# Parameter rows loaded in pairs, and late rounding, roots, evictions and table loads moved in a two-block transformer kernel

## The reference

```python
# first block, for each layer l
h = rmsnorm(x, g_mix[l]);  proj = h @ w_in[l]           # 1024 -> 6656
# proj: gates, a gated 31-tap convolution, and three attentions (neighbourhood, dilated, windowed)
x = x + sum(sigmoid(gate + gate_b) * (y_n @ w_branch[l, n]) for n in range(4)) @ w_out[l]
u = depthwise_conv(rmsnorm(x, g_ffn[l]) @ w_up[l]);     x = x + (silu(gate) * up) @ w_down[l]
# second block, for each layer l; cs is a second stream of 256 context tokens
m = silu(c) @ w_mod[l] + b_mod[l]                       # 1024 -> 9216, one row for x, one for cs
x, cs = half ffn step, modulated by m[0:3]
p = modulate(rmsnorm(x, mix_norm[l]), m[3:6]) @ w_in[l] # Fourier part, 3-tap conv part, q, kv, rope
x = x + m[5] * (concat(fourier, conv, latent attention over x and cs) @ w_out[l])
x = half ffn step, modulated by m[6:9]                  # cs likewise, but not in the last layer
```

## Time and profile before

| | |
|---|---|
| median of 3 runs | 2647.29 us (2644.49 to 2649.88) |
| the profiled execution's own time | 2649.91 us |
| its span in the trace | 2648.1 us |
| TensorE (PE) busy | 2568.1 us, 97% |
| VectorE (DVE) busy | 1483.0 us, 56% |
| ScalarE (ACT) busy | 1028.8 us, 39% |
| GpSimd (POOL) busy | 55.1 us, 2% |
| mean granted clock of TensorE | 0.994 of 2.4 GHz |

### The profile page before, as it was taken

How to read it: one execution, slowest core, us unless ns; L and a number is a source line. 1 busy time by engine, 2 the same in 40 slices (tenths; PEclk the granted TensorE clock), 3 DMA queues, 4 the chain that set the end, 5 groups by cost and what they waited for, 6 DMA issues and landing times.

```text
span 2648.1 us, 48248 instructions
## 1 busy us (share of the span) xinstructions
PE 2568.1 (97%) x20320; PEld 2263.5 (85%) x20320; DVE 1483.0 (56%) x2156; ACT 1028.8 (39%) x1408; POOL 55.1 (2%) x76
## 2 busy tenths in 40 slices
PE   7999999999999999999999999999999999998999
PEld 6998999899899978888876688888888888876999
DVE  6787786777878653333525563333553334545656
ACT  4545564545455432222324432122332122345433
POOL 2003000000100000000000000000000000000000
PEclk8999999999999999999999999999999999999999
DMA  8577766667675642532436342432532532556673
GB/s 222 169 243 175 210 179 184 194 204 211 192 209 166 198 113 85 144 91 76 145 87 185 111 123 80 133 103 71 143 97 87 144 86 81 168 157 188 173 202 118
DMA packets 613848, 393.66 MB, mean 149 GB/s; under 512 B 47470, under 2 KB 609428, under 8 KB 613539
## 3 DMA queue, kind: packets, MB, share of 16 engines
q1 hardware_dynamic: 610623, 383.31, 50.0%
q0 software_dynamic: 2176, 6.42, 1.0%
q10 hardware_dynamic: 868, 1.31, 0.2%
HBM read 389.94 MB, written 1.05 MB: 148 GB/s over the span
## 4 chain that ended last, share of the span: by engine, by line
PE 89%; DVE 6%; ACT 2%; issue 1%; POOL 1%; DMA 1%; DVEq 1%; ACTq 0%
PE acc L1002 12%; PE acc L1004 12%; PE acc L1003 12%; PE scores L1002 6%; PE scores L1003 6%; PE scores L1004 6%; PE scores L1065 3%; PE scores L1066 3%; PE scores L1067 3%; PE acc L1065 3%; PE acc L1066 3%; PE acc L1067 3%; PE stat L1195 2%; DVE hf L2171 1%; DVE wlo L2091 1%
## 5 line engine op out<-in xcount | busy, mean ns | idle before, releaser
L1541 ACT ACTIVATE whi<-raw 128x2048 fp32r<-128x2048 f32 (+3 forms) x346 | 569.0, 1647 | 824.5 <-PE acc L1004 251.3
L2091 DVE TENSOR_TENSOR wlo<-raw,whi 128x2048 fp32r<-128x2048 f32 (+2 forms) x306 | 629.0, 2056 | 214.1 <-ACT whi L1541 213.3
L1002 PE MATMUL acc<-h,whi 128*128 128x512 f32 (+1 forms) x988 | 355.1, 359 | 8.0 <-DVE u L2692 4.6
L1004 PE MATMUL acc<-h,wlo 128*128 128x512 f32 (+1 forms) x988 | 353.1, 357 | 1.6 <-issue 1.6
L1003 PE MATMUL acc<-h,whi 128*128 128x512 f32 (+1 forms) x988 | 353.1, 357 | 0.0
L1002 PE MATMUL acc<-h_hi,whi 128*128 128x256 f32 x1056 | 302.0, 286 | 2.9 <-DVE cg L2573 1.6
L1003 PE MATMUL acc<-h_lo,whi 128*128 128x256 f32 x1056 | 295.8, 280 | 0.0
L1004 PE MATMUL acc<-h_hi,wlo 128*128 128x256 f32 x1056 | 295.5, 280 | 0.0
L1002 PEld LDWEIGHTS acc<-h,whi 128*128 128x128 f32 x988 | 186.9, 189 | 38.9 <-DVE u L2692 5.3
L1002 PE MATMUL scores<-h,whi 128*128 128x512 f32 (+1 forms) x608 | 219.0, 360 | 1.0 <-DVE wlo L2091 1.0
L1003 PE MATMUL scores<-h,whi 128*128 128x512 f32 (+1 forms) x608 | 218.9, 360 | 0.0
(11 more groups left out here) (395 smaller groups left out, 5192.9 us busy)
## 6 DMA issues: line engine op xcount, KB each, us to landing
raw<-in_ffn_w_in_dram SPq DMA_DIRECT2D x176, 512.0 KB, 5.1
raw<-in_w_mod_dram SPq DMA_DIRECT2D x72, 1024.0 KB, 5.3
raw<-in_w_in_dram SPq DMA_DIRECT2D x62, 1024.0 KB, 5.6
raw<-in_w_up_dram SPq DMA_DIRECT2D x88, 512.0 KB, 5.1
raw<-in_ffn_w_out_dram SPq DMA_DIRECT2D x64, 704.0 KB, 4.7
raw<-in_w_down_dram SPq DMA_DIRECT2D x32, 704.0 KB, 4.7
raw<-in_w_out_dram SPq DMA_DIRECT2D x16, 1024.0 KB, 7.2
raw<-in_w_branch_dram SPq DMA_DIRECT2D x16, 512.0 KB, 6.3
```

Of the source, the lines that this page charges most:

```text
L1002: pe.matmul(bank, wh, hi[:, c0 + k, 0:width], start=(k == 0), stop=False)
L1004: ins = pe.matmul(bank, wl, hi[:, c0 + k, 0:width], start=False, stop=(k == ph.shape[0] - 1))
L1541: return act.activation(out_, in_, ACT.Copy, **kw)
L2091: dve.tensor_tensor(wlo[:, s % 2, 0:el], raw[:, slot, 0:el], f32(whi[:, s % 2, 0:el]), ALU.subtract).then_inc(s_lo, 1)
```

## The change

The parameter arrays are loaded for both layers in one DMA (`both`), in another order of rows; the six pairs of head gains (64 wide) are loaded with both halves and both layers in one DMA. Block 0 now holds exactly 128 rows of 8 loads. The third unit of the phases behind a norm (e = 2) is rounded and subtracted in two halves, as the first was before, and so is the unit of 2.1.kv. The sum of squares of the very first norm is made whole on VectorE, which saves TensorE two matmuls. The rest moves instructions: the places of modulation units, `IN_AMONG`, the eviction of 2.x.in's unit 2 in the last layer, the wait of q01, the Silu of `cond`, `load_sqrt`, the root of the kv norm, and the `rpb` loads of layer 1, which now wait until tile 16 of 1.0.up. Cut to its core:

```diff
-MID_MODS = ((2, 2, 1), (2, 2))
-PAIR_MODS = ((2, 0, 2, 0, 2, 0, 0, 0, 0, 0, 0, 0, 2, 1), (2, 0, 2, 0, 1, 0, 0, 0, 2, 1))
+MID_MODS = ((3, 2, 1), (2, 2))
+PAIR_MODS = ((2, 0, 2, 0, 1, 0, 0, 0, 0, 0, 0, 0, 3), (2, 0, 2, 0, 1, 0, 0, 0, 3))
+TAIL_MODS = 2
-IN_AMONG = (9, 12, 15)
+IN_AMONG = (8, 11, 14)
+        self.halved = {0: True, 2: n > 2} if self.behind_norm else {0: name == f"2.{DEPTH - 1}.kv"}
...
+    def both(k, view):
+        ap = A[k].rearrange(view, p=P)
+        first, each = sum(r.shape[0] for r in rows), ap.shape[0] // DEPTH
+        for l in range(DEPTH):
+            column[(k, l)] = first + l * each
+        rows.append(ap)
...
@@ gpsimd @@
+                if l:
+                    pool.wait_ge(s_accfree, by_name[f"1.{l - 1}.up"].t0 + 16)
                 base = A["na_rpb"][l]
...
@@ tensor @@
+                    elif free is not None:
+                        pe.wait_ge(s_accfree, free)
...
-                pe.wait_ge(s_accfree, by_name[nm + "q01"].t0)
-                unit(nm + "q01", 0, None, h2_hi, h2_lo, T, plain(256))
+                unit(nm + "q01", 0, None, h2_hi, h2_lo, T, plain(256), free=by_name[nm + "in"].t0 + 6)
...
                         pair_weigh(k - 2, pairs[k - 2])
+                    given = SITES["pair", l, k] if k < len(pairs) else []
+                    for lu in given:
+                        mod_unit(*lu)
                     if 0 <= k - 1 < len(pairs):
                         pair_turn(k - 1, pairs[k - 1])
-                    for lu in SITES.get(("pair", l, k), []):
-                        mod_unit(*lu)
+                    if k == len(pairs):
+                        for lu in SITES["pair", l, k][:TAIL_MODS]:
+                            mod_unit(*lu)
+                for lu in SITES["pair", l, len(pairs)][TAIL_MODS:]:
+                    mod_unit(*lu)
...
@@ scalar @@
-                if e == 0 and to.behind_norm:
+                if to.halved.get(e):
...
-                load_sqrt()
                 for j in range(DC):
                     round_next(name, j, None)
+                    if j == 0:
+                        load_sqrt()
...
                     if e + DC == IN_AMONG[2]:
+                        act.wait_ge(s_pad2, 2 * (l + 1))
+                        in_out(2)
                         round_next(nm + "in", 3, None)
...
-                take_root(kv_norm)
                 for seg in range(nseg):
...
+                    if seg == 0:
+                        take_root(kv_norm)
...
@@ vector @@
-            dve.tensor_tensor(wlo[:, 0, 0:half], raw[:, 0, 0:half], ...).then_inc(s_head_lo, 1)
+            head_low(0)
+            flatten(norm_x(1, ("g_mix", 0), h1_hi, h1_lo))
+            head_low(1).then_inc(s_head_lo, 1)
...
-                if e == 1:
+                if e == 3:
...
-                if e in (4, 6):
+                if e in (5, 7):
```

More of the change, by code:

```diff
@@ L344, in param @@
         rows.append(ap)
+    def both(k, view):
[4 more added lines that the diff above has]
+        rows.append(ap)
     def vec(x):
         return x.rearrange("(c p) -> c p", p=P)
[L349 to L363, removed]
+    flat, taps_ = "l (c p) -> (l c) p", "l k (c p) -> (l k c) p"
+    both("g_mix", flat)
+    both("gate_b", taps_)
+    for k in ("a_conv_b", "a_ln_g", "a_ln_b", "g_ffn", "ffn1_norm_2", "kv_norm_2"):
+        both(k, flat)
+    both("a_conv_w", taps_)
+    both("ffn_conv_w", taps_)
+    both("ffn_conv_b", flat)
+    for k in ("na_qn", "na_kn", "dil_qn", "dil_kn", "swa_qn", "swa_kn"):
+        for l in range(DEPTH):
+            column[(k, l)] = sum(r.shape[0] for r in rows) + l
+        rows.append(A[k].rearrange("l (a d) -> l a d", a=1).broadcast_to([DEPTH, 2, DH]))
     param("c", vec(A["c_2"][0]))
     param("c_ctx", vec(A["c_ctx_2"]))
+    for k in ("mix_norm_2", "ffn2_norm_2", "q_norm_2", "b_mod_2"):
+        both(k, flat)
+    both("conv_w_2", taps_)
     param("final", vec(A["final_norm_2"]))
@@ L376, in build @@
             take = min(n - done, P - p0)
[L377 to L380, removed]
+            pieces.append((b, p0, take, r[done:done + take]))
             done += take
@@ L975, in parted, with unit @@
                     ins.then_inc((s_accx, s_acc)[seg], 1)
-            def unit(name, j, i, hi, lo, width, weights, c0=0, ring=2, upto=None):
+            def unit(name, j, i, hi, lo, width, weights, c0=0, ring=2, upto=None, free=None):
                 ph = by_name[name]
@@ L1215, in turn_rows @@
                 turn([prow[0:min(P, n_rows - b * P), b, :] for b in blocks])
[L1217 to L1219 removed]
             pe.wait_ge(s_sum, 7)
[L1221 removed]
+            pe.matmul(stat[:, 0:SEQ], ones, rstd[:, 0:SEQ], start=True, stop=True).then_inc(s_sum, 1)
             n("sum", 8)
@@ L1825, in _ @@
                             squares(norm_heads(l, p))
+                    if l == 0 and name == "nak":
+                        act.wait_ge(s_condzero, 1)
+                        act.wait_ge(s_turned, 4 + row_turns)
+                        for s, key in enumerate(("c", "c_ctx")):
+                            a = column[key]
+                            act.activation(cond[:, :, s:s + 1], par[:, a:a + DC].rearrange("p (c a) -> p c a", a=1),
+                                           ACT.Silu).then_inc(s_cond, 1)
                 def gate_out(gate):
```

48 lines of the change are left out of this document (26 added, 22 removed).

## The result

The changed kernel takes 2627.60 us (median of 4 runs, 2625.93 to 2630.69), beside 2646.79 of the kernel before: ratio 0.9932, with a 95% interval of 0.9920 to 0.9943. It is faster by 19.2 us in the medians. The prediction had said 2616 and a range of 2609 to 2627, so the sign is right, the time is 11.6 us above the forecast, and it lies 0.6 us above the range. The profiled execution took 2626.78 us, its span is 2624.6: 23.5 less than the span before.

A forecast was written before the change was run, and what follows sets the result against it. TensorE, 97% busy, bounds the kernel: its work at its clock plus some 80 us standing. Terms summed to 32.2 us off the profiled 2649.9: 2617.7, or 2615.1 from the median; said 2616, own range 2610 to 2621, whole range 2609 to 2627.

The forecast's parts named there:

- The eviction of `u` and the earlier rounding in 2.1.in: 2.1.in: q01 starts 4.2 us earlier, 3.0 of half clock and 0.8 of kv's wait go; 8.0 us, bounds 4.2 and 8.5.
- Bias loads: 1.0.out: TensorE's 3.0 us wait goes when layer 1's `rpb` loads move into 1.0.up; 3.0 us, bounds 0 and 3.0.
- q01 of 2.0: 2.0: q01 no longer waits for VectorE's product; 0.8 us.
- Halves: Unit 2 of 1.x.up: halved rounding and subtracting brings VectorE's taps 0.8 us earlier, twice; 1.6 us, bounds 0.8 and 1.6.
- Parameter rows: Turn of the rows: with fewer loads the 5.8 us wait and 2.3 of half clock go; 8.1 us, bounds 0 and 8.5.
- nothing waits: Parameter rows: the Silu of `cond`, moved behind nak, lies beside nav and dilq's two flips and delays nothing; its cost there about 1.3.
- Fourier parts: Eviction `fab` ahead of ScalarE's root removes waits of 2.0 and 0.8 and 1.7 half clock; 4.2 us, bounds 2.5 and 4.5.
- Attention: A modulation unit fills the turn's wait in step 4 of 2.0 (1.8); tail waits for `mods` go (3.1); 4.9 us.
- First norm: First norm: VectorE adds for 0.6 us, TensorE loses two matmuls, VectorE's total is the same; 0.3 us, bounds 0 and 1.1.
- half clock: 1.2 GHz stretches behind long waits go: 2.3 at the rows, 1.7 in the Fourier part, 3.0 in 2.1.in; rival 'stays', chance 0.13.
- the sign that I had named for being wrong: The clock falls at other places, since it is granted by what TensorE does; no size given.
- new waits: Rival: VectorE or a load is late where no cost was counted; 6 to 10 us fewer, 2622 to 2626, chance 0.12.

The follow-up runs named there:

- run 11: The changed kernel with 2.1.in in the old order (rounding places, unit 2's eviction, q01 waiting for `u`), halved units kept: 2632.99 us.
- run 7: The changed kernel with the 16 bias loads of layer 1 beside 1.0.out again, as before the change: 2629.62 us.
- Run 2: The changed kernel with VectorE's wait for the table `t` moved ahead of its part of nav: 2625.05 us.
- run 3: The changed kernel with two modulation units instead of three in the first Fourier segment of 2.0, the missing one moved to attention step 4: 2620.33 us.
- run 9: The changed kernel with two matmuls on constants added on TensorE at the start, VectorE's part of the norm edit kept: 2624.24 us.
- run 13: The kernel of run 8 with two small matmuls on constants added at the start: 2615.94 us, ratio 0.9885 to the kernel before.
- run 8: The changed kernel with VectorE's table wait moved ahead of nav and two modulation units in the first Fourier segment of 2.0: 2617.74 us.
- run 6: The changed kernel with the first norm's sum and the split of the head's low weights as before the change: 2624.07 us.
- run 5: The kernel before the change once more, no edit, for a second trace: 2647.27 us.
- run 1: The changed kernel once more, no edit, for a second trace: 2627.06 us.
- runs 14 and 15: The kernel of run 8 with ten and with eighteen small matmuls on constants at the start: 2614.86 us and 2618.12 us.
- run 10: The kernel of run 3 with the attention's modulation units behind the turn again, as in the kernel before: 2621.98 us.

## Why the prediction was too low

*The steps that held.* The eviction of `u` and the earlier rounding in 2.1.in: forecast 8.0, measured 7.8 and 6.5 in two pairs of traces and 5.9 by undoing the order alone (run 11); the wait became 1.58 where I had said 1.5, at full clock. Bias loads 3.0: 2.6 in the medians (run 7), 3.2 and 6.0 in the traces. The table load in 1.1.down1 1.3: 1.4. q01 of 2.0: 1.1 for 0.8. Halves: 0.8 in 1.0.up and 0.7 to 0.8 in 1.1.up (740 to 745), as counted; by 750, 0.5 of the second is left. Fourier part of 2.1: 0.9 for 0.8. Nothing waits for `mods` at the tails. In 1.0.out 0.56 us stay ahead of the first unit, where I had said none above 0.3; it was 0.53 before.

*Parameter rows, 8.1.* The step that failed is "nothing waits". I worked out a chain of 5.2 us for nak's weights, ScalarE and VectorE, and held it against 5.3; VectorE was not free to run it, since a wait for `t` stood in its program, and `t` landed at 38.7 and not at 34.5 as before. I had seen that SyncE would be done before the table's load, and not that the loads of weights behind it would then run beside it. Run 2 shows the 8.1 with that wait moved.

*Fourier parts, 4.2.* The step that failed is "I take off 0.3, because the fifth modulation unit is now loaded ahead of uq's second unit". It was 1.8 to 3.2 us in the seven traces with the third unit in place. I took the third unit for harmless, because I asked what it filled and not which load it made the next one; and with the eviction ahead of the root two units were cover enough (run 3).

*Attention, 1.8 + 3.1.* The tail is right. The turn is not: I had VectorE ready at 1457.8 and named it as the bound of these steps, and still counted the whole 1.8. With the unit in front TensorE waited 1.25 at this turn and 1.52 at the next. Timeline of PE in the changed kernel:

```profile
1442.84 1.09 PE L1187 MATMUL turns<-shared,lat 128*128 128x128 f32 x8 [1.25 <-DVE lat L2318]
...
1448.59 1.09 PE L1187 MATMUL turns<-shared,lat 128*128 128x128 f32 x8 [1.52 <-DVE lat L2318]
```

*First norm, 0.3.* The step that failed is that TensorE loses two matmuls at no cost elsewhere: with 8 instructions fewer it stood for want of instructions 100 us later. No term of mine had such a cost, and no rival. It is 2.8 us by run 9 and 1.8 by run 13 against run 8 (1.6 and 0.7 if each run is held against the kernel before on its chip), and 1.2 to 2.4 as the stop in the seven traces that have it. The term itself was too small: the first stage is about 1.3 us shorter (run 6), since VectorE's "total is the same" was asserted and not worked out.

*The clock.* I had counted 7.0 us of half clock as gone (2.3, 1.7, 3.0). It went for good in 2.1.in, in all thirteen traces with the new order there. In the other places it was never sure: run 5 had none in the Fourier part before the change, and runs 2 and 6 have some after it. And the sign that I had named for being wrong, the clock falling at other places, came too (269.6 and 918.1 us in run 1). The terms are chances, and I had taken what one execution showed.

In medians: run 13 takes 2615.9, the changed kernel 2627.6, and the prediction said 2616. The three defects (6.7, 2.0 and 2.8 measured singly, which make 11.5; 11.1 from run 1 to run 13) are as large as the 11.6 us that were missing. That run 13 lands on 2616 is in part luck: the 6.7 holds up to 1.7 us of stops that were in no term, the first norm gave 1 us more than its term, the stop of 1.62 us at 2424.85 went by itself, and the turn (1.8) and part of the clock (7.0) did not come as counted. The rival "new waits", 2622 to 2626 with a chance of 0.12, was the case that came, and both places that it named first had such a wait; its price was too small by 1.6 us, and 0.12 was a low chance for it.

Three slips of the prediction weigh little. The list of TensorE's waits was read as one large wait and a tail at places that the change touches; the full list also has 8.0 in five waits for `h_lo`, 5.4 for the first table and 4.5 for `prt`, most of which it does not touch. The terms of 2.1.in give 2306.8 and not 2306.6 for q01, 0.2 less gain. And the sum of all upper bounds is 35.3, so 2612 from the median: the lower end of the range, 2609, follows from no sum.

What stays open: why 8 instructions decide whether the fetch comes 2.2 to 3.3 us ahead of the block (3.8 and 6.1 in runs 14 and 15) or 0.7 to 1.7 us inside it (seven of the eight traces with the lower count have it inside, none of the nine with more; the eighth, run 10, has it ahead), and what the order of turn and modulation unit is worth.

## What to carry to other kernels

When a long wait is taken away, read every wait of the engines behind it that had ended below it, the ones for transfers first: the next stop is the one that was hidden, and it need not be on the engine whose chain was worked out. A filler put into a gap uses up something, here a loaded slot, so look where the next one of its kind is due before it is called free. A change of the instruction count alone can move a stop into a dense run of small matmuls, so judge an edit worth under 3 us by undoing it, not by its own place in the trace.

## What the runs showed that I had not expected

Queue q8 carries 139 or 140 fetches of 16 KB in a run, in the median 250 traced instructions of TensorE apart. Two matmuls more or fewer move the places where TensorE stands, so I take the fetches for TensorE's instructions. A block of two modulation units is 256 instructions in 2.0 us. In the seventeen traces together TensorE stood 52 times for more than 0.15 us at a record that waits for no semaphore, 45 of them inside a block of 128 modulation records, and each time it went on 1.2 to 1.6 us after the last fetch had landed. A fetch takes 0.9 to 2.6 us, 1.1 in the median. The place of a stop goes with the count: seven traces stop behind record 120 of the block at 112 to 116 us, with the fetch starting anywhere from 0.7 to 1.7 us into it, and the later it starts the longer they stand (1.15 to 2.42 us). A fetch that starts inside a block is not enough, though: 194 blocks of 128 had one in their first 1.75 us and no stop. The profile calls such a stop "issue", and also calls other waits so. I had passed over the 1.62 us at 2424.85 before the prediction as a gap in the records; it was such a stop (a fetch landed at 2425.10), 2.42 us long in run 5 and absent in the changed kernel.

Two matmuls on constants, added while TensorE waits, made the kernel faster by 2.8 us in the medians (1.6 by the kernel before on the same chip), by their number only.
